# Delta rule in chunks: from a product w = U'(decayed k) to a subtraction of the decayed k'S from the values

## What is computed

```python
sol = lax.linalg.triangular_solve(lower, rhs, left_side=True, lower=True, unit_diagonal=True)
u, w = sol[..., :A_DV], sol[..., A_DV:]
def step(S, inp):
    qk_i, qd_i, kd_i, u_i, w_i, gl_i = inp
    v_new = u_i - w_i @ S
    o = qd_i @ S + qk_i @ v_new
    S = S * gl_i + kd_i.T @ v_new
```

## Time and profile before

| | |
|---|---|
| median of 3 runs | 1531.24 us (1530.87 to 1532.17) |
| span of the profiled execution | 1528.9 us |
| TensorE busy in the span | 1509.2 us, 99% |
| VectorE busy | 920.3 us, 60% |
| ScalarE busy | 735.1 us, 48% |
| GpSimd busy | 257.7 us, 17% |
| granted TensorE clock | 1.000 over the span |

### The profile page before, as it was taken

One profiled execution on the slowest core, in us unless ns is written; L12 is line 12 of the kernel. 1 busy time (PEld: TensorE's weight loads), 2 busy tenths in 40 slices (PEclk: granted clock), 3 DMA queues, 4 the chain that ended last, 5 costly groups with the idle time before them and its releaser, 6 DMA issues.

```text
span 1528.9 us, 21108 instructions
## 1 busy us (share of the span) xinstructions
PE 1509.2 (99%) x7848; PEld 1211.0 (79%) x7848; DVE 920.3 (60%) x1733; ACT 735.1 (48%) x1284; POOL 257.7 (17%) x446
## 2 busy tenths in 40 slices
PE   9999999999999999999998999999999999999998
PEld 7878888888888877877876887666778888888887
DVE  5767777787654566677778445554475243433467
ACT  4454455544553346655667234566555241332343
POOL 2044334444312003433341000000000000000000
PEclk9999999999999999999999999999999999999999
DMA  5321111111114232222221231111222222222221
GB/s 207 110 70 51 61 56 56 56 56 56 45 57 152 97 112 89 84 71 73 87 84 55 101 107 64 56 69 56 69 89 104 87 98 107 93 100 95 99 83 69
DMA packets 40165, 127.25 MB, mean 83 GB/s; under 512 B 4576, under 2 KB 9104, under 8 KB 40064
## 3 DMA queue, kind: packets, MB, share of 16 engines
q1 hardware_dynamic: 38112, 121.65, 23.1%
q0 software_dynamic: 1040, 3.27, 0.6%
q10 hardware_dynamic: 912, 0.99, 0.2%
HBM read 122.69 MB, written 2.15 MB: 82 GB/s over the span
## 4 chain that ended last, share of the span: by engine, by line
PE 89%; ACT 5%; DVE 3%; issue 2%; DMA 0%; POOL 0%; SPq 0%; DVEq 0%; ACTq 0%; POOLq 0%
PE ps L884 87%; PE ps L1263 1%; PE ps L1029 1%; ACT wh L1407 1%; ACT L L1820 1%; DVE wl L2018 1%; ACT L1832 1%; ACT L1400 1%; DVE L L2560 1%; ACT L L1781 0%; ACT xreg L1832 0%; ACT sp L1914 0%; DVE up L2172 0%; ACT sp L1912 0%; ACT pT L1841 0%
## 5 line engine op out<-in xcount | busy, mean ns | idle before, releaser
L884 PE MATMUL ps<-xr,wh 128*128 128x512 f32 x2720 | 871.6, 401 | 1.8 <-DVE xr L2609 0.9
L884 PEld LDWEIGHTS ps<-xr,wh 128*128 128x128 f32 x2720 | 498.9, 188 | 123.6 <-issue 26.1
L884 PE MATMUL ps<-xr,wl 128*128 128x512 f32 x1376 | 537.6, 391 | 0.0
L2018 DVE TENSOR_TENSOR wl<-wraw,wh 128x1024 fp32r<-128x1024 f32 x214 | 261.5, 1230 | 134.2 <-ACT wh L1407 133.2
L884 PEld LDWEIGHTS ps<-xr,wl 128*128 128x128 f32 x1376 | 258.2, 188 | 55.8
L1407 ACT ACTIVATE wh<-wraw 128x1024 fp32r<-128x1024 f32 x214 | 222.0, 1048 | 74.4 <-PE ps L884 73.1
L884 PE MATMUL ps<-xm,wh 128*128 128x512 f32 x640 | 197.8, 390 | 0.0
L884 PEld LDWEIGHTS ps<-xm,wh 128*128 128x128 f32 x640 | 119.5, 188 | 26.2 <-DVE xm L2695 1.6
L884 PE MATMUL ps<-xm,wl 128*128 128x512 f32 x320 | 124.5, 389 | 0.0
L2869 POOL TENSOR_SCALAR L<-L,m 128x256 f32<-128x256 f32 (+1 forms) x120 | 90.6, 774 | 189.0 <-DVE m L2575 189.0
L2056 DVE SCALAR_TENSOR_TENSOR qkv<-cin,gains,qkv 128x512 f32<-128x512 f32 x96 | 85.5, 892 | 9.7 <-ACT qkv L1437 8.9
(11 more groups left out here) (283 smaller groups left out, 1773.2 us busy)
## 6 DMA issues: line engine op xcount, KB each, us to landing
wraw<-in_wa SPq DMA_DIRECT2D x48, 512.0 KB, 3.2
wraw<-in_wb SPq DMA_DIRECT2D x32, 512.0 KB, 3.8
wraw<-in_wu SPq DMA_DIRECT2D x32, 512.0 KB, 3.2
wraw<-in_wd SPq DMA_DIRECT2D x32, 512.0 KB, 3.2
wraw<-in_wao SPq DMA_DIRECT2D x16, 512.0 KB, 3.2
wraw<-in_wbo SPq DMA_DIRECT2D x16, 512.0 KB, 3.6
wraw<-in_wc SPq DMA_DIRECT2D x16, 512.0 KB, 3.3
bias<-rel_rows SPq DMA_DIRECT2D x16, 256.0 KB, 3.9
```

The source lines that it names most:

```text
L884: return e.matmul(out, w, x, start=start, stop=stop, skip_group_check=True)
L2018: e.tensor_tensor(m.wl[:, i % N_SPLIT, :], m.raw[:, i % N_RAW, :], m.wh[:, i % N_SPLIT, :].bitcast(F), ALU.subtract).then_inc(s.wlo, 1)
```

## The change

The w product is gone: U no longer multiplies the decayed keys, and `kg`, its VectorE operation, the copy `wT` and their semaphores go with it. Instead each chunk n > 0 begins with a step k(n): TensorE forms k'S from the kept keys `kc` and S into the free half of bank 4; VectorE multiplies it by -exp(g) (`egn`) and adds it to the values in place (`vt`); then r(n) is U times these values alone. `recur` has 14 steps instead of 11. The normed keys are written to their own tile `kc`, two heads deep, since they must live until the recurrence. The `PLAN` strings of rounds 2 to 9 are rewritten. ScalarE's `gate_z` for head 6 stands one step earlier, in k(3) instead of r(3).

```diff
-    "a2": plan("p0 p5 p2 q0 p2 q4 q1 q2 q0 p0 q2 q0 p2 q0 p3 r0 p1 r0 r1 p0 r0 r1 p1 r0 r3 r0 r0 p4 r0 p0 p4 p0 r6"),
-    "a8": plan("p0 q2 p0 q3 q1 q1 p0 q0 p3 q0 p0 q0 p1 q0 p1 r1 r0 r1 p0 r0 r0 p2 p0 r0 p0 p0 r3 r4 r0 p0 p0 r1 r2"),
-    "a9": plan("q1 q5 q2 q5 q2 q1 q3 q7 r7 r0 r1 r0 r2 r0 r2 r1 r3 r2 r4"),
-    "a": plan("p0 q2 q0 p4 q1 q0 p1 p0 q3 q2 p0 q1 p0 q2 p0 r2 r2 r0 p2 r0 p2 r1 p0 p2 r2 r1 r2 r1 p1 r2 p2 p2 r14"),
+    "a2": plan("p0 p5 p2 q0 p2 q4 q1 q2 q0 p0 q2 q0 p1 q0 p2 r1 p0 r0 r1 r1 p0 r0 r1 r1 p0 r0 r1 r1 r1 r0 p3 r0 p0 p4 p0 r6"),
+    "a8": plan("p0 q2 p0 q3 q1 q1 p0 q0 p2 q0 p0 q1 p0 q0 p0 r1 r0 r1 r1 p0 r0 r1 p0 r1 p0 r0 p0 r1 p0 r2 r2 r0 p0 p0 r1 r2"),
+    "a9": plan("q1 q5 q2 q5 q2 q1 q3 q0 r6 r1 r1 r1 r1 r2 r2 r1 r2 r2 r1 r3 r2 r4"),
+    "a": plan("p0 q2 q0 p4 q1 q0 p1 p0 q3 q2 p0 q2 p0 q0 p0 r1 r2 r0 p2 r1 r0 p2 r1 r1 p0 r0 p2 r1 r2 r2 r1 p1 r2 p2 p2 r4"),
...
-        e.wait_ge(s.lev_v, lev_v(h, "U6"))
-        end(four(bank(), lambda n: m.kg[:, n, :], lambda n: U[:, n, :]), (s.lev_a, lev_a(h, "w")))
         yield
...
             if n == 0:
-                e.wait_ge(s.lev_a, lev_a(h, "w"))
-            ins = mm(m.banks[4][:, 0:256], m.U[:, par, n, :], m.vt[:, par, n, :], True, n == 0)
-            if n:
-                e.wait_ge(s.rec_v, REC_V * h + n)
-                ins = mm(m.banks[4][:, 0:256], m.wT[:, par, n, :], so, False, True)
-            ins.then_inc(s.rec_p, 1)
+                e.wait_ge(s.lev_v, lev_v(h, "U6"))
+                e.wait_ge(s.prep_a, prep_a(h, "v1"))
+            else:
+                e.wait_ge(s.rec_v, rec_v(h, f"S{n}"))
+                mm(m.banks[4][:, 256:512], m.kc[:, par, ts], so).then_inc(s.rec_p, 1)
+                yield
+                e.wait_ge(s.rec_v, rec_v(h, f"v{n}"))
+            mm(m.banks[4][:, 0:256], m.U[:, par, n, :], m.vt[:, par, n, :]).then_inc(s.rec_p, 1)
...
-        e.wait_ge(s.lev_p, lev_p(h, "w"))
-        if h >= 2:
-            e.wait_ge(s.rec_p, REC_P * (h - 2) + 11)
-        did(e.activation(m.wT[:, h % 2], o, ACT.Copy))
...
-        did(e.tensor_tensor(k, k, m.rq[:, 0, :], ALU.mult))
+        free_of_recurrence()
+        did(e.tensor_tensor(m.kc[:, par, :], k, m.rq[:, 0, :], ALU.mult))
...
-        did(e.tensor_tensor(m.kg[:], o, bc(m.egn[:, col]), ALU.mult))
         did(e.tensor_tensor(m.kd[:, par], o, bc(m.ekd[:, col]), ALU.mult))
...
+            if n:
+                v = m.vt[:, h % 2, n, :]
+                e.wait_ge(s.rec_p, rec_p(h, f"k{n}"))
+                did(e.scalar_tensor_tensor(out=v, in0=m.banks[4][:, 256:512], scalar=m.egn[:, 4 * h + n:4 * h + n + 1],
+                                           in1=v, op0=ALU.mult, op1=ALU.add))
+                yield
```

More of the change, by code:

```diff
@@ L314 @@
 }
-STEPS = {"gates": 4, "prep": 14, "levels": 8, "recur": 11, "kv_post": 4, "attend": 9, "attend2": 9, "split_o": 1, "split_ob": 1,
+STEPS = {"gates": 4, "prep": 14, "levels": 8, "recur": 14, "kv_post": 4, "attend": 9, "attend2": 9, "split_o": 1, "split_ob": 1,
          "stick0": 12, "stick1": 14, "ple": 8, "post": 8}
@@ L586, in __init__ @@
         self.qd = a.new([2, 512], name="qd")
-        self.kg = a.new([4, 128], name="kg")
         self.kd = a.new([2, 4, 128], name="kd")
         self.vt = a.new([2, 4, 256], name="vt")
-        self.wT = a.new([2, 4, 128], name="wT")
+        self.kc = a.new([2, 512], name="kc")
         self.U = a.new([2, 4, 128], name="U")
@@ L799 @@
     ("silu1", "sqk", "silu0", "silu2", "silu3", "lnk", "exk", "eb", "E", "sqq", "v0", "v1"))}
-PREP_V = {n: i + 1 for i, n in enumerate(("dv", "y", "at", "qk", "kg", "kd", "dc", "qdn", "U3", "T3"))}
+PREP_V = {n: i + 1 for i, n in enumerate(("dv", "y", "at", "qk", "kd", "dc", "qdn", "U3", "T3"))}
 PREP_O = {n: i + 1 for i, n in enumerate(("sel", "D"))}
 N_INV = 31
-LEV_P = {n: i + 1 for i, n in enumerate(("P4", "U4", "P5", "U5", "T5", "P6", "U6", "w"))}
-LEV_A = {n: i + 1 for i, n in enumerate(("P4", "P5", "T5", "P6", "w"))}
+LEV_P = {n: i + 1 for i, n in enumerate(("P4", "U4", "P5", "U5", "T5", "P6", "U6"))}
+LEV_A = {n: i + 1 for i, n in enumerate(("P4", "P5", "T5", "P6"))}
 LEV_V = {n: i + 1 for i, n in enumerate(("U4", "T4", "U5", "U6"))}
 LEV_O = {n: i + 1 for i, n in enumerate(("M4", "M5", "M6"))}
-REC_P, REC_A, REC_V = 12, 8, 9
+REC_P = {n: i + 1 for i, n in enumerate(
+    ("r0", "d0", "o0", "k1", "r1", "d1", "o1", "k2", "r2", "d2", "o2", "k3", "r3", "o3", "sum"))}
+REC_V = {n: i + 1 for i, n in enumerate(("S1", "v1", "S2", "v2", "S3", "v3", "q0", "q1", "g0", "g1", "f0", "f1"))}
+REC_A = 8
 STICK_P = {n: i + 1 for i, n in enumerate(
@@ L844, in lev_o, with rec_p, rec_v @@
     return len(LEV_O) * h + LEV_O[name]
+def rec_p(h, name):
+    return len(REC_P) * h + REC_P[name]
+def rec_v(h, name):
+    return len(REC_V) * h + REC_V[name]
 def stick_p(j, name):
@@ L1655, in recur @@
                 tables()
-            e.wait_ge(s.rec_p, REC_P * h + 3 * n + 1)
+            if n:
+                yield
+            e.wait_ge(s.rec_p, rec_p(h, f"r{n}"))
             if n >= 2:
-                e.wait_ge(s.rec_p, REC_P * h + 3 * (n - 2) + 3)
+                e.wait_ge(s.rec_p, rec_p(h, f"o{n - 2}"))
             elif h:
-                e.wait_ge(s.rec_p, REC_P * (h - 1) + 11)
+                e.wait_ge(s.rec_p, rec_p(h - 1, "o3"))
             did(e.activation(m.rr[:, n % 2], m.banks[4][:, 0:256], ACT.Copy))
@@ L1664, in recur @@
         for j in range(2):
-            e.wait_ge(s.rec_p, REC_P * h + 11)
+            e.wait_ge(s.rec_p, rec_p(h, "o3"))
             if h:
-                e.wait_ge(s.rec_v, REC_V * h)
+                e.wait_ge(s.rec_v, rec_v(h - 1, "f1"))
             did(e.activation(m.sqh[:, j, :], m.banks[6 + j][:], ACT.Square))
         yield
-        e.wait_ge(s.rec_p, REC_P * h + 12)
+        e.wait_ge(s.rec_p, rec_p(h, "sum"))
         if h == 0:
@@ L1694, in square @@
             e.wait_ge(s.olo, 16)
-            e.wait_ge(s.rec_p, REC_P * HEADS)
+            e.wait_ge(s.rec_p, len(REC_P) * HEADS)
             e.wait_ge(s.prep_o, len(PREP_O) * HEADS)
@@ L2323, in free_of_recurrence @@
             if h >= 2:
-                e.wait_ge(s.rec_p, REC_P * (h - 2) + 11)
+                e.wait_ge(s.rec_p, rec_p(h - 2, "o3"))
         yield from idle(3)
@@ L2418, in recur @@
             if n < 3:
-                e.wait_ge(s.rec_p, REC_P * h + 3 * n + 2)
+                e.wait_ge(s.rec_p, rec_p(h, f"d{n}"))
                 if n:
-                    e.wait_ge(s.rec_p, REC_P * h + 3 * (n - 1) + 3)
-                    e.wait_ge(s.rec_v, REC_V * h + n)
+                    e.wait_ge(s.rec_p, rec_p(h, f"o{n - 1}"))
+                    e.wait_ge(s.rec_v, rec_v(h, f"S{n}"))
                     did(e.scalar_tensor_tensor(out=sn, in0=so, scalar=m.egl[:, 4 * h + n:4 * h + n + 1],
```

25 lines of the change are left out of this document (12 added, 13 removed).

## The result

The changed kernel takes 1545.47 us (median of four executions, 1544.26 to 1548.82) against 1531.1 for the kernel before beside it: a ratio of 1.0091, 95% interval 1.0076 to 1.0106. The direction was as forecast; the size was not: +6.6 us forecast, +14.4 measured, and the time lies above the upper end of the range (1543). The profiled execution has a span of 1543.6 us, 14.7 more than before. (One execution of the kernel before, at 1638.5 us with a granted clock of 0.872, stood apart from all others and is left out of every comparison.)

The account below looks back on a forecast made before the run. TensorE was taken as the bound, busy 99% of the span. Waits of 7.8 + 1.8 + 3.1 + 1.1 = 13.8 us less the 7.2 gain made +6.6: 1531.24 becomes 1537.8 us, range 1528 to 1543.

Parts of the forecast that it names:

- The w product, 0.90 us a head: Dropping this eight-record TensorE product saves 0.90 us in each of eight heads, 7.2 us in all.
- Rounds 3 to 7, +0.66 a round: Waits of 1.55 us a round, 7.8 in five rounds; the period becomes 47.0 + 0.66 us.
- kT: TensorE waits between qk and kT for VectorE's qkT: 1.0 us in rounds 3 to 8, 0.35 in round 2.
- the three k and r turns: Rounds 3 to 7: waits of 0.15 us from r(1) to d(1), 0.15 at k(2), 0.25 at k(3).
- VectorE is just free for qkT: Rounds 3 to 7: VectorE reaches qkT about when the qk product is ready, so kT waits only 1.0 us.
- Round 9, +0.2: Waits of 1.1 us: 0.8 at k(1), 0.35 together at k(2), k(3) and r(1).
- the bare k step: A k with no TensorE step before its r, at k(3) in round 2 and k(1) in round 9: 0.8 us each.
- Round 2, 1.8 us of waits forecast: Waits: kT 0.35, d(0) to k(1) 0.3, k(1) and k(2) 0.3 together, k(3) 0.8, r(3) to o(3) 0.05.
- VectorE becomes the bound: Rival, chance 0.05: k(1) to k(3) each lose 0.5 us in VectorE's queue, 12 us more, 1550 us.
- Round 8, 3.1 us forecast: Waits: kT 1.0, S(1) 0.3, k(1) and k(3) 0.3, the sum 1.2, gate 0.6; less 0.3 already lost.
- The gate's 0.6: Round 8: gate_z holds ScalarE 3.76 us between r(2) and r(3); a wait of 0.6, from nothing to 0.8.
- The clock falls: Rival, chance 0.03: short waits take the clock to 1.2 GHz for one round, which could double; 1560 us or more.

Follow-up runs that it names:

- quarter run: The kernel before with the w product left out for three of the four chunks of each head: 1525.8 us, ratio 0.9969.
- masks later: The kernel after with GpSimd's two mask products of the next head held until VectorE's last addition of the head before: 1545.4 us, ratio 1.0074.
- long-wait run of the kernel before: The kernel before with four filler steps fewer ahead of round 8's sum, run at the round's end instead: 1534.9 us, ratio 1.0021.
- second new order: The kernel after with the filler steps laid anew in all four strings, second try: 1537.7 us; also run with mask products held: 1534.7, and qkT earlier too: 1537.9.

## Why the prediction fell short, step by step

Two steps failed. The waits of rounds 2 and 8 were priced by the length of each hop; the queue of VectorE ahead of it, and GpSimd's work beside it, stood nearly at nothing. Each round lost 2.8 us more than forecast (1.6 of it in round 8 is the clock). And the clock stood at nothing in the sum, where it cost 3.2 us.

- **The w product, 0.90 us a head: right** (0.89 by the quarter run).
- **Rounds 3 to 7, +0.66 a round: right** (+0.73), and right term by term. kT was forecast at 1.0 and lost 1.0; the three k and r turns were forecast at 0.55 and came to 0.57 (0.11 at d(1), 0.15 at k(2), 0.31 at k(3)). That VectorE is just free for qkT was right too.
- **Round 9, +0.2: right**; the bare k step cost what was forecast: k3 at 455.03, its product with U at 456.20, 1.17 us where 0.33 would do, so 0.84 lost against 0.8 forecast.
- **Round 2, 1.8 us of waits forecast, 4.6 lost (+3.7 net of the gain): the step failed.** Counted by the distances of starts, bare k(3) came as forecast (0.84 against 0.8), and k(1) and k(2) with 0.3; kT lost 0.60 (forecast 0.35), S(1) 0.81 (0.3), o(3) 0.50 (0.05). The sum was not in the forecast at all and lost 1.4, 1.16 of it as a wait: a wait of over 1 us that was not named is one of the prediction's own signs of being wrong. Its chain was laid out in round 8 but never in round 2, where the weight split on VectorE (142.78) took 1.92 us instead of 1.23. S(1) was late because kd, dc and five shuffles stand ahead of it in VectorE's queue. With the masks later this round was 0.5 us shorter (51.50 against 52.04), so that much of it is the collision. In the form of the forecast: at these hops only the hop's own length was priced, not the queue in front of it. That is the rival "VectorE becomes the bound" (0.05), true in two rounds instead of all.
- **Round 8, 3.1 us forecast, about 5.9 measured: the terms of the sum and of kT were mis-sized.** Forecast 1.2 us at the sum, measured 2.18: 1.0 of it is the collision (masks later); the rest is close, since the chain is 3.7 us and not 3.35, but 2.55 and not 2.27 us of work lie under it. kT lost 1.55 us (qk at 408.07, kT at 410.51, less 0.89), not 1.0: the split of weights ahead of qkT took 1.73 us, again beside GpSimd (a copy and a mask product on it at 407.49 to 409.95). The forecast said "no GpSimd instruction is added" and left it there; that they would move against VectorE's was not asked. The gate's 0.6 came to 0.3: o(3) lost 0.41 us against 0.13 before, since ScalarE's copy of r(3) (424.05) stands behind a table load. Against these, the two waits that TensorE lost there before, 0.85 us and not 0.3, are gone. 1.6 us is the clock.
- **"The clock falls" (0.03) happened**, in two places and not for a whole round: 1.6 us behind the sum's wait of 2.18, and 1.6 us behind the sqr wait at 592.76, which grew from 1.69 to 1.96 us. None of the four executions had the full clock, while 36 of 57 of the kernel before did. For the first there is support: it went when the wait was shortened, in two profiles, and the long-wait run of the kernel before has it. The second is only argued: a fall follows that wait in six profiles (1.96 to 2.0 us), but in the three of the second new order the wait is 2.0 us long and no fall follows.
- **Outside the span**: 2.3 us were added for what lies around it, the execution shows 1.8 (1545.42 less 1543.6), as all the others do whose span is listed; 0.5 us the other way. The 2.3 was a median less the span of a different execution.
- **The lower end of the range of the reading**, 10.1 us of waits, is not the sum of the terms named for it, which come to about 9. Nothing of the forecast hangs on it.

The pieces: 6.6 forecast, +2.8 in round 2, +2.8 in round 8, +0.4 in rounds 3 to 7, +2.2 behind the delta rule, less 0.1 ahead of the delta rule, are the 14.7 of the span. Of these errors, which come to 8.1, 3.2 us are the clock and some 1.5 the collision (1.0 in round 8 and 0.5 in round 2 by its edit). Of the other 3.4, 2.3 lie in round 2: the sum's chain that was left out, and hops that VectorE's queue made late. That is read from the rows and was not tested by an edit of its own.

## What to carry to other kernels

A product taken off the bounding engine also takes cover away; before counting the gain, lay every hop of the new order against the queue of the engine that it crosses, in each round that has its own string, and not against the hop's length alone. In that queue look for long operations that nobody waits for now and ask what they run beside: here a stretch of 1 us a time, harmless while it hit a tap, cost 19.7 us, with the clock behind it, when an order put it ahead of the sum in six rounds. And judge small changes at equal granted clock: a ratio of 1.0006 hid 1.4 us.

## What the hardware showed that was not expected

- VectorE's 128x512 fp32 additions took 0.69 us, and 1.72 to 1.79 when GpSimd's 128x512 product had begun just before; a pair of taps 1.53 and 2.61; a weight split 1.23 and 1.73 to 1.92. Taking the overlap away gave 1.0 us back at the sum of round 8 and in each of rounds 3 to 6 of the second new order, and 0.5 in round 2 of the kernel after.
- In the profiled executions the granted clock went to 1.2 GHz for 3.4 us behind waits of 2.18 and 2.54 us, behind four of five of 2.17 and six of nine of 1.96 to 2.0, and not behind 1.69. What decides stays open.
- Another fall, of 6.8 us, stood at one place of the program in eight of thirteen profiles and fits the 3.2 us by which 21 of 57 executions of one and the same kernel were longer. The waits just ahead of it (0.57 and 0.41 to 0.50 us) are there with and without it.
